# 115 semaphore increments ahead of TensorE's program in a hybrid layer with sixteen experts

## What is computed

```
affin = softmax(xt @ w_router)
gates, idx = top_k(affin.T, cap)          # cap: 128 latent and 32 context tokens an expert
xs = xt[idx]
hid = silu(einsum('ecd,edf->ecf', xs, w_gate)) * einsum('ecd,edf->ecf', xs, w_up)
y = einsum('ecf,efd->ecd', hid, w_down) * gates[..., None]
out = zeros_like(xt).at[idx].add(y)
```

## Time and profile before

| | us |
|---|---|
| median of 3 runs | 3904.4 (3903.5 to 3906.6) |
| the profiled execution, its own time | 3897.1 |
| its span, first to last instruction | 3895.4 |
| TensorE busy | 3418.8 |
| expert loop on TensorE | 2037.8 to 3818.3 |
| one pass of it | 110.5 to 114.5 |

### The profile page before, as it was taken

One profiled execution on the slowest core, in us unless ns is written; L12 is line 12 of the kernel. 1 busy time (PEld: TensorE's weight loads), 2 busy tenths in 40 slices (PEclk: granted clock), 3 DMA queues, 4 the chain that ended last, 5 costly groups with the idle time before them and its releaser, 6 DMA issues.

```text
span 3895.4 us, 51888 instructions
## 1 busy us (share of the span) xinstructions
PE 3418.8 (88%) x20875; PEld 3064.1 (79%) x20875; DVE 2206.0 (57%) x2396; ACT 1715.3 (44%) x1853; POOL 528.4 (14%) x581
## 2 busy tenths in 40 slices
PE   6899999997899788986859999999999999999991
PEld 4677777784578666874649999999999999999991
DVE  5633343455743375333857666666666666666664
ACT  5633433553332233222325555555555555555552
POOL 1063053002300122003010000000000000000001
PEclk8999999998999699986969999999999999999996
DMA  8855455673043212421647878877877877877876
GB/s 274 287 182 180 172 191 186 216 277 131 30 173 119 100 33 105 145 96 54 216 156 242 254 245 254 253 248 243 253 256 244 251 248 250 252 242 257 255 233 240
DMA packets 542061, 783.32 MB, mean 201 GB/s; under 512 B 15680, under 2 KB 408944, under 8 KB 529408
## 3 DMA queue, kind: packets, MB, share of 16 engines
q1 hardware_dynamic: 507072, 616.60, 48.2%
q0 software_dynamic: 34752, 163.10, 12.7%
HBM read 713.51 MB, written 66.13 MB: 200 GB/s over the span
## 4 chain that ended last, share of the span: by engine, by line
PE 74%; DVE 10%; ACT 5%; issue 4%; DMA 4%; POOL 3%; DVEq 0%; ACTq 0%; POOLq 0%
PE PS L723 29%; PE PS L533 12%; PE PS L725 11%; PE PS L657 9%; PE PS L615 2%; DVE wlo L1052 2%; DVE lo_f L1294 2%; PE PS L681 2%; ACT whi L796 1%; PE PS L630 1%; PE PS L600 1%; PE PS L671 1%; PE PS L480 1%; PE PS L481 1%; DMA arena_ab<-k_rope 1%
## 5 line engine op out<-in xcount | busy, mean ns | idle before, releaser
L1294 DVE TENSOR_TENSOR lo_f<-raw_f,hi_f 128x2048 fp32r<-128x2048 f32 x384 | 878.4, 2292 | 505.2 <-ACT hi_f L981 504.9
L723 PE MATMUL PS<-xT,hi_f 128*128 128x320 f32 x4096 | 1093.4, 354 | 71.4 <-issue 39.6
L725 PE MATMUL PS<-xT,lo_f 128*128 128x160 f32 x4096 | 981.8, 240 | 0.0
L723 PEld LDWEIGHTS PS<-xT,hi_f 128*128 128x128 f32 x4096 | 792.8, 194 | 75.6 <-issue 75.4
L725 PEld LDWEIGHTS PS<-xT,lo_f 128*128 128x128 f32 x4096 | 806.1, 197 | 0.0
L1052 DVE TENSOR_TENSOR wlo<-raw,whi 128x2048 fp32r<-128x2048 f32 x204 | 472.8, 2336 | 564.3 <-ACT whi L796 563.8
L981 ACT ACTIVATE hi_f<-raw_f 128x2048 fp32r<-128x2048 f32 x384 | 732.0, 1910 | 81.1 <-PE PS L725 70.5
L796 ACT ACTIVATE whi<-raw 128x2048 fp32r<-128x2048 f32 x204 | 387.0, 1917 | 474.9 <-PE PS L657 187.9
L723 PE MATMUL PS<-hid,hi_f 128*128 128x320 f32 x2048 | 533.6, 346 | 0.0
L725 PE MATMUL PS<-hid,lo_f 128*128 128x160 f32 x2048 | 482.8, 236 | 0.0
L725 PEld LDWEIGHTS PS<-hid,lo_f 128*128 128x128 f32 x2048 | 390.8, 191 | 0.0
(11 more groups left out here) (243 smaller groups left out, 4658.9 us busy)
## 6 DMA issues: line engine op xcount, KB each, us to landing
raw_f<-w_gate SPq DMA_DIRECT2D x128, 1024.0 KB, 5.5
raw_f<-w_up SPq DMA_DIRECT2D x128, 1024.0 KB, 6.0
raw_f<-w_down SPq DMA_DIRECT2D x128, 1024.0 KB, 5.7
raw<-w_ada SPq DMA_DIRECT2D x96, 1024.0 KB, 5.3
raw<-w_in SPq DMA_DIRECT2D x60, 1024.0 KB, 5.6
raw<-w_out SPq DMA_DIRECT2D x48, 1024.0 KB, 5.2
arena_cd<-mod_rows POOLq DMA_DIRECT2D x9, 1024.0 KB, 7.3
arena_ab<-x_sample POOLq DMA_DIRECT2D x8, 1024.0 KB, 9.8
```

The lines of the kernel that those rows point to most:

```text
L723: nc.tensor.matmul(PS[:, b + m, 0:2 * CAP], hi_f[:, n % NSPL_F, r, w], x, start=(kt == 0), stop=False, skip_group_check=True)
L725: ins = nc.tensor.matmul(PS[:, b + m, 0:CAP], lo_f[:, n % NSPL_F, r, w], x[:, 0:CAP], start=False, stop=(kt == last_kt), skip_group_check= ...
L1294: nc.vector.tensor_tensor(lo_f[:, n % NSPL_F], raw_f[:, n % NRAW_F], hi_f[:, n % NSPL_F].bitcast(F32), ALU.subtract).then_inc(f_lo_ok, 1)
```

## The change

It adds one semaphore and, at the beginning of TensorE's program, 115 empty instructions that each raise it by one. Nobody waits for that semaphore. All later instructions of TensorE lie 115 places further back in its program, the loop's 1,662 among them; blocks of 256 instructions are counted from the program's start. The change's own description says that the loop then lies in seven such blocks.

```diff
+PE_PAD = 115
@@
-        rtab_in = sem("rtab_in")
+        rtab_in, pe_pad = sem("rtab_in"), sem("pe_pad")
@@
+            for _ in range(PE_PAD):
+                pe.nop().then_inc(pe_pad, 1)
             pe.wait_ge(consts_in, 16 * N_CONST)
             pe.wait_ge(cond_in, 48)
```

## The result

The changed kernel takes 3788.9 us, median of four runs from 3783.7 to 3797.8; the kernel before has 3904.0 us in the same comparison. The ratio is 0.971, with a 95% interval of 0.969 to 0.973. The forecast was 3794 us in a range of 3783 to 3836. The execution whose profile is shown is the slowest of the four, 3797.8 us.

What follows compares the result with a forecast made beforehand. The prediction took TensorE, busy for 88% of the span, as the bound, with its largest loss at the loop's back edge. Stall 70.4 us plus clock 40 us, pads and supply 0, took 3904.4 to 3794 us, range 3783 to 3836.

Steps and rivals of the forecast that it cites:

- What the gap is: At the loop's back edge, TensorE's 5.07 us without work is its sequencer's branch of 5.28 us, not the wait named `lo_f`.
- The branch becomes short: At the loop's end, seven blocks and one fetched ahead stay resident, so no fetch and a branch of some 0.06 us.
- The Trainium skill's rule of a two-page window: Support for the rival that the loop's branch still waits for its target's fetch: 3904 us, chance 0.10.
- the estimate in the prediction: TensorE's instruction memory of 128 KB would be eight lines of 16 KB, exactly the seven and the one ahead.
- The body begins at 141: Without pads the loop's 1,662 instructions begin at place 141 of a 256-instruction block and touch eight; 115 pads make it seven.
- The stall, 70.4 us: TensorE's 15 waits at the loop's back edges vanish, the branch lying beside the transposes; saving 70.4 us.
- the fourth piece: The next pass's fourth piece of weights, there at 2147.55 and wanted at 2156.2, so not late.
- The clock, 40 us: After each restart in the loop TensorE's granted clock no longer falls; 40 us regained, of 40.7 us lost.
- Supply: In the shorter loop pass of 104.2 us the DMA's mean rises from 250 to 268 GB/s; cost taken as 0.
- The pads at nothing: At the start, 115 pads of 51 ns take 5.9 us, hidden under TensorE's idle to 14.76 us; cost 0.
- The sum: Over the whole kernel, 70.4 + 40 = 110 us saved, giving 3794 us.
- The clock's rival: In the loop the stall goes but the clock doesn't come back: 3834 us, chance 0.04.

Runs made afterwards that it cites:

- the longer body: The changed kernel with 115 pads plus 128 empty instructions in each pass, making the body 1,790 instructions; 3897.3 us, 0.996 to 1.000 of the kernel before.
- a body of 1,693 instructions: The changed kernel with 115 pads plus 31 empty instructions at the end of each pass; 3891.7 us, 0.994 to 0.997 of the kernel before.

## Why the prediction was right, step by step

*What the gap is: the sequencer's branch, not `lo_f`.* Right. The waits named `lo_f` went when the fetches went, and came back under that name with empty instructions in the branch's place.

*The branch becomes short, since seven blocks and one ahead are kept.* Right in the result, and the longer body shows that it hangs on how far the body reaches. That old blocks are kept was inferred from DVE's queue in the prediction; the runs add that TensorE, with 115 pads, keeps a body of 1,693 instructions and not one of 1,790. That the limit is eight blocks with one of them ahead remains the reading that fits, not a measured number. The Trainium skill's rule of a two-page window (Runtime: NRT & Kernel Launch, Instruction fetch mechanics) would have given 3904 us and doesn't hold here: queue 8 brings no block between 2158 and 3615 us. The Trainium skill's 128 KB for TensorE (Advanced Engine Details and Errata, ISA Cache) fit the runs, eight blocks of 16 KB by the estimate in the prediction; the same section's "Only 2 cache lines!" doesn't fit them.

*The body begins at 141.* Wrong. This step took the figure from the number of pads. It begins at 145 to 240, and the change works because any start within 131 of the 256 places will do, not because it aligns the loop. For this step the forecast was lucky: 115 pads hit that window anyway. The same step did fail where it mattered, for the body 128 instructions longer (3789 us expected, 3897.3 measured).

*The stall, 70.4 us.* Right, and 15 x 0.25 = 3.7 us too low, because the new pass now begins ahead of the last transpose's end. The branch took 0.21 us and not 0.06, which is still hidden. A slip that changed nothing: from a start at 2143.4 the fourth piece would be wanted at 2155.7, not at 2156.2.

*The clock, 40 us.* Right: the first two pieces of a pass take 8.26 us in place of 10.89, 15 x 2.63 = 39.4 us. Stall, overlap and clock are 113.5 of the 113.7 us that the loop lost.

*Supply.* Right: 267 GB/s, share 0.85, no wait for `lo_f`, as worked out (268).

*The pads at nothing.* Wrong by 3.8 us. I took the length of a record, 51 ns, and twice that as the upper end; the distance from one to the next is 151 ns. The prediction had 0.128 us as the point where the cover ends, so the cover was passed, by 18.53 - 14.76.

*The sum.* The loop's 113.7 us less the pads' 3.8 are 109.9 us, beside the 110 of the forecast: the errors of the terms nearly cancel. The medians are 115.1 us apart (105 to 121 by the interval of the ratio). The 5 us between lie within the spread of the executions, and no run assigns them.

The clock's rival (3834 us) has its mechanism in the kernel with eight pads at the end: 0.75 us more of idle, and the fall would have been there in part.

## What to carry to other kernels

If a wait at a loop's edge is put down to a semaphore that had long been signalled, look at the loop's own line for the branch's length, and at the instruction queue's transfers in one pass. A long body can be fetched anew in every pass because it reaches one block too far; try pads in front, at several shifts, since the place counted in the program was not the true one. Pads at the very start are hidden only as long as the engine waits there anyway. And an idle of some 4 us in a loop of multiplications can cost over half its length again in clock.

## What the runs showed that I had not expected

The profile's record of an empty instruction is 51 ns, and its cost to TensorE's sequencer 151 to 155 ns when they follow each other; between multiplications 128 of them a pass cost nothing that shows. A taken branch of TensorE whose target is there takes 208 ns, against 45 to 56 ns on ScalarE and VectorE. And passes of the resident loop repeat to 0.01 us from the second on (104.06 to 104.07; the first has 105.7), while those with fetches spread over 110.5 to 114.5: most of the loop's unsteadiness came from the fetch and the clock.
